# Differential attention in the even mixer: units 3 to 5 steps apart, and the second map scaled on ScalarE

## The reference

```python
def diff_attention_group(q, k, v, pos, layer, lambdas, subln):
    ...                                   # rope on q and k, 8 heads, two maps each of 64 dimensions
    lam = exp(sum(lf[0] * lf[1])) - exp(sum(lf[2] * lf[3])) + lam_init
    def block(start, q1b, q2b):           # 128 queries at a time
        mask = chunk_causal_mask(start, s)
        p1 = masked_softmax(einsum('bqhd,bkhd->bhqk', q1b, k1) * scale, mask)
        p2 = masked_softmax(einsum('bqhd,bkhd->bhqk', q2b, k2) * scale, mask)
        return einsum('bhqk,bkhe->bqhe', p1 - lam * p2, vf)
    o = sweep_query_blocks(block, q1, q2)
    return rms_norm(o, subln) * (1.0 - lam_init)
```

## Time and profile before

| | us |
|---|---|
| median of 3 runs | 2914.96 (2914.41 to 2916.4) |
| profiled execution, span | 2910.3 |
| around the span (median less span) | 4.7 |
| PE busy | 2814.2 |
| DVE busy | 1394.9 |
| ACT busy | 846.7 |
| POOL busy | 1355.7 |

### The profile page before, as it was taken

One profiled execution on the slowest core, in us unless ns is written; L12 is line 12 of the kernel. 1 busy time (PEld: TensorE's weight loads), 2 busy tenths in 40 slices (PEclk: granted clock), 3 DMA queues, 4 the chain that ended last, 5 costly groups with the idle time before them and its releaser, 6 DMA issues.

```text
span 2910.3 us, 36762 instructions
## 1 busy us (share of the span) xinstructions
PE 2814.2 (97%) x14588; PEld 2179.5 (75%) x14588; DVE 1394.9 (48%) x2266; ACT 846.7 (29%) x1575; POOL 1355.7 (47%) x1106
## 2 busy tenths in 40 slices
PE   7999999999989999999999999999999988999997
PEld 5888777777878877677886666788787755788886
DVE  3321656766563122435846777523725956511113
ACT  3011432331131143322336233232233225222222
POOL 3344323324534643558766543844545412744443
PEclk9999999999999999999999999999999989999999
DMA  7112222222321221233221112232323320332322
GB/s 269 44 44 66 66 66 94 69 78 94 122 76 59 68 77 58 73 101 119 87 73 57 57 47 73 76 101 83 105 81 100 126 59 16 118 99 86 103 85 74
DMA packets 244821, 243.81 MB, mean 84 GB/s; under 512 B 5376, under 2 KB 234624, under 8 KB 244032
## 3 DMA queue, kind: packets, MB, share of 16 engines
q1 hardware_dynamic: 243360, 237.96, 25.2%
q0 software_dynamic: 1312, 3.80, 0.5%
HBM read 233.22 MB, written 7.34 MB: 83 GB/s over the span
## 4 chain that ended last, share of the span: by engine, by line
PE 82%; DVE 11%; issue 2%; ACT 2%; POOL 1%; SPq 1%; DMA 1%; DVEq 0%; ACTq 0%; POOLq 0%
PE psum L933 22%; PE psum L935 21%; PE psum L934 21%; PE psum L1203 4%; PE psum L1182 1%; PE psum L1138 1%; DVE columns L2640 1%; PE psum L1158 1%; PE psum L1320 1%; PE psum L1137 1%; POOL columns L3352 1%; PE psum L1207 1%; DVE columns L2913 1%; PE psum L1471 1%; SPq L774 1%
## 5 line engine op out<-in xcount | busy, mean ns | idle before, releaser
L933 PE MATMUL psum<-columns,columns 128*128 128x512 f32 (+1 forms) x3464 | 1347.6, 389 | 12.6 <-POOL columns L3352 5.0
L935 PE MATMUL psum<-columns,columns 128*128 128x512 f32 (+1 forms) x3464 | 1263.2, 365 | 0.0
L934 PE MATMUL psum<-columns,columns 128*128 128x512 f32 (+1 forms) x3464 | 1261.7, 364 | 0.0
L3352 POOL TENSOR_TENSOR columns<-columns,columns 128x512 fp32r<-128x512 f32 (+1 forms) x676 | 912.3, 1379 | 436.6 <-ACT columns L1867 403.3
L3348 POOL TENSOR_TENSOR columns<-columns,columns 128x512 fp32r<-128x512 f32 x392 | 419.1, 1100 | 1011.0 <-PE psum L935 805.9
L933 PEld LDWEIGHTS psum<-columns,columns 128*128 128x128 f32 x3464 | 654.9, 189 | 196.1 <-issue 77.3
L934 PEld LDWEIGHTS psum<-columns,columns 128*128 128x128 f32 x3464 | 655.6, 189 | 124.3 <-issue 28.3
L935 PEld LDWEIGHTS psum<-columns,columns 128*128 128x128 f32 x3464 | 653.9, 189 | 111.5
L1867 ACT ACTIVATE columns<-columns 128x1024 fp32r<-128x1024 f32 (+2 forms) x154 | 136.7, 935 | 172.3 <-PE psum L935 165.8
L2640 DVE SCALAR_TENSOR_TENSOR columns<-columns,columns,columns 128x256 f32<-128x256 f32 x224 | 154.7, 745 | 0.0
L2622 DVE SCALAR_TENSOR_TENSOR columns<-columns,psum 128x512 f32<-128x512 f32 x80 | 54.7, 684 | 184.4 <-PE psum L1203 181.9
(11 more groups left out here) (414 smaller groups left out, 2754.8 us busy)
## 6 DMA issues: line engine op xcount, KB each, us to landing
columns<-in_w_merge SPq DMA_DIRECT2D x32, 1024.0 KB, 6.5
columns<-in_w_ada SPq DMA_DIRECT2D x24, 1024.0 KB, 5.7
columns<-in_w_in SPq DMA_DIRECT2D x22, 1024.0 KB, 5.1
columns<-in_ev_w_in SPq DMA_DIRECT2D x22, 1024.0 KB, 5.0
columns<-in_ffn_gate SPq DMA_DIRECT2D x22, 1024.0 KB, 5.2
columns<-in_ffn_up SPq DMA_DIRECT2D x22, 1024.0 KB, 5.2
columns<-in_ffn_down SPq DMA_DIRECT2D x16, 768.0 KB, 4.6
columns<-in_ffn_down SPq DMA_DIRECT2D x16, 640.0 KB, 4.1
```

What stands on the lines that cost most here:

```text
L933: mm(dst, weights(0, k), moving(0, k), start=start and k == 0, stop=False)
L934: mm(dst, weights(0, k), moving(1, k), start=False, stop=False)
L935: last = mm(dst, weights(1, k), moving(0, k), start=False, stop=stop and k == k_tiles - 1)
L3352: last = g.tensor_tensor(low[:, c], raw[:, c], high[:, c].bitcast(F32), ALU.subtract)
```

## The change

The fixed distance of 4 steps goes. The units start at 36 + 16h + (0, 3, 7, 11): three steps after unit 0 of a head, four after units 1 and 2, five from unit 3 to the next head. `turn` stays 8 steps and `mix` 11 steps behind. The exps are issued two steps after the scores. `swap` and `rope` of every second tile (n odd) stand at k = 1 in place of 2. The copy of a head's output, its square, its sum and what follows stand some steps further from `mix`, and since the units begin sooner and the last one starts at step 159 in place of 164, they are at about the same places as before or some steps earlier.

The scaling of the second map leaves DVE. `inverses(u)` on DVE inverts both sums and multiplies the second one's inverse by the factor; `scale(u)` on ACT multiplies the second map with it; `weights(u)` on DVE waits for that and adds. DVE's list at the start of unit u is now inverses(u - 1), maxima(u), weights(u - 1).

```diff
-UNIT_AT, UNIT_STEPS, TURN, MIX = 40, 4, 8, 11
+UNIT_STARTS = [36 + 16 * h + (0, 3, 7, 11)[i] for h, i in UNITS2]
+EXPS, TURN, MIX, LAST_WEIGHTS = 2, 8, 11, UNIT_STARTS[-1] + 5
...
-    return head_mixed_at(3) + 7 + 3 * h if h < 4 else head_mixed_at(7) + 7 + 2 * (h - 4)
+    return head_mixed_at(3) + 9 + 3 * h if h < 4 else head_mixed_at(7) + 9 + 2 * (h - 4)
...
-                    if k == 2 and 1 <= n <= 16:
+                    if k == 2 - n % 2 and 1 <= n <= 16:
                         swap(n - 1)
                     for h in range(8):
-                        if step == head_mixed_at(h) + 3:
+                        if step == head_mixed_at(h) + 5:
                             sub_sum(h)
...
+                def scale(u):
+                    n = (UNITS2[u][1] + 1) * P
+                    p = pr_diff[0][:, u % 2, 1, 0:n]
+                    act.wait_ge(total_inverted, UNITS0[2] + u + 1)
+                    f(p, p, ACT.Identity, scale=cols[:, 5 + 2 * (u % 2):6 + 2 * (u % 2)]).then_inc(prob_weighed, 1)
...
+                    u = unit2_at(step, 0)
+                    if u:
+                        scale(u - 1)
+                    if step == LAST_WEIGHTS:
+                        scale(len(UNITS2) - 1)
...
-                    u = unit2_at(step, 0)
+                    u = unit2_at(step, EXPS)
                     if u is not None:
                         exps(u)
                     for h in range(8):
-                        if step == head_mixed_at(h):
+                        if step == head_mixed_at(h) + 3:
                             act.wait_ge(o2_used, h + 1)
...
-                        if h % 4 == 3 and step == head_mixed_at(h) + 4:
+                        if h % 4 == 3 and step == head_mixed_at(h) + 6:
                             sub_root(h // 4)
...
-                def weights(u):
-
-                    n = (UNITS2[u][1] + 1) * P
+                def inverses(u):
                     c = cols[:, 4 + 2 * (u % 2):6 + 2 * (u % 2)]
                     dve.wait_ge(p2_ready, u + 1)
                     order(v.reciprocal(c, c))
+                    v.tensor_scalar(c[:, 1:2], c[:, 1:2], lamw[:, 5:6], None, ALU.mult).then_inc(total_inverted, 1)
+
+                def weights(u):
+
+                    n = (UNITS2[u][1] + 1) * P
+                    c = cols[:, 4 + 2 * (u % 2):6 + 2 * (u % 2)]
                     p = pr_diff[0][:, u % 2, :, 0:n]
-                    order(v.tensor_scalar(p[:, 1], p[:, 1], c[:, 1:2], lamw[:, 5:6], ALU.mult, ALU.mult))
+                    dve.wait_ge(prob_weighed, UNITS0[2] + u + 1)
...
                     u = unit2_at(step, 0)
                     if u is not None:
+                        if u:
+                            inverses(u - 1)
                         maxes(u)
                         if u:
                             weights(u - 1)
...
-                        if step == head_mixed_at(h):
+                        if step == head_mixed_at(h) + 2:
                             dve.wait_ge(mixed2, 4 * h + 4)
```

More of the change, by code:

```diff
@@ L308, in unit2_at @@
 def unit2_at(step, phase):
-    u = step - UNIT_AT - phase
-    return u // UNIT_STEPS if u >= 0 and u % UNIT_STEPS == 0 and u // UNIT_STEPS < len(UNITS2) else None
+    return UNIT_STARTS.index(step - phase) if step - phase in UNIT_STARTS else None
 def head_mixed_at(h):
-    return UNIT_AT + UNIT_STEPS * (4 * h + 3) + MIX
+    return UNIT_STARTS[4 * h + 3] + MIX
 def spread_at(h):
-    return head_mixed_at(3) + 7 + 3 * h if h < 4 else head_mixed_at(7) + 7 + 2 * (h - 4)
+    return head_mixed_at(3) + 9 + 3 * h if h < 4 else head_mixed_at(7) + 9 + 2 * (h - 4)
 OD_TILES = (4, 5, 6, 7, 8, 9, 0, 1, 2, 3)
@@ L2914, in maxes @@
                     v.tensor_scalar(c, c, -0.125, None, ALU.mult).then_inc(maxed2, 1)
+                def inverses(u):
+                    c = cols[:, 4 + 2 * (u % 2):6 + 2 * (u % 2)]
+                    dve.wait_ge(p2_ready, u + 1)
+                    order(v.reciprocal(c, c))
+                    v.tensor_scalar(c[:, 1:2], c[:, 1:2], lamw[:, 5:6], None, ALU.mult).then_inc(total_inverted, 1)
                 def weights(u):
@@ L2962, in ev_qk_out @@
                             weights(u - 1)
-                    if step == UNIT_AT + UNIT_STEPS * len(UNITS2):
+                    if step == LAST_WEIGHTS:
+                        inverses(len(UNITS2) - 1)
                         weights(len(UNITS2) - 1)
                     for h in range(8):
-                        if step == head_mixed_at(h):
+                        if step == head_mixed_at(h) + 2:
                             dve.wait_ge(mixed2, 4 * h + 4)
                             v.tensor_copy(qk2[:, h, :], psum[:, 7 * BANK:8 * BANK]).then_inc(o2_used, 1)
-                        if h % 4 == 3 and step == head_mixed_at(h) + 4:
+                        if h % 4 == 3 and step == head_mixed_at(h) + 6:
                             dve.wait_ge(sub_summed, h + 1)
```

2 lines of the change are left out of this document (removed).

## The result

The changed kernel takes 2923.8 us (median of 11 runs, 2920.7 to 2926.9), the kernel before 2916.0 on the same chip (11 runs, 2914.0 to 2918.7): ratio 1.0024, 95% interval 1.0016 to 1.0032. It is slower by 7.8 us. The prediction said 2923.0.

A forecast was written before the change was run, and what follows sets the result against it. TensorE, busy 97%, was taken as the bound, with 23.5 us at most to gain. Pauses of 26.5 us instead of 20.2 (6.3 more) plus 1.7 for the clock gave 8.0: 2914.96 + 8.0 = 2923.0 us, range 2910 to 2932.

The forecast's parts named there:

- (5): Start, first unit at step 36: TensorE waits 5.9 us behind VectorE's gate-norm multiply and first maxima, 4.5 us more.
- (3): GpSimd's windows, steps 48 to 96: one wait of 2.4 us each before unit 3's transposes, instead of 2.1 in two.
- (4): Odd tiles' ropes one step earlier: swap waits 0.15 us for ScalarE's copy, eight times, 1.2 us; lower end 0.
- (6): Later windows: 3.2 us lost at step 112, 4.6 at 128, 2.0 at 144, none at 160.
- (1): Second map's scaling on ScalarE: at most 0.72 us per unit, costing nothing as long as VectorE's maxima last longer.
- (2): One-column multiply added on VectorE per unit: 0.2 us and no wait for GpSimd; bounds 0.15 and 0.98.
- One fall more than before: Clock falls behind the start, step 112 and step 128, three instead of two: 1.7 us more.
- are nearer to 1.99 than to 2.90: Window waits of 2.4 us (shown as 2.3) bring no clock fall; a 1.99 pause kept full speed, 2.90 did not.
- The fall behind step 112: One of three expected clock falls, behind the waits at step 112 that add up to about 3.2 us.
- the rival of the clock in each window: Five more clock falls, behind four waits of 2.3 us and one of 2.0: 8.5 us, 2931 us; chance 15%.
- The faster rival: Unit 3's chain leaves GpSimd's window, saving 1.8 us in each of six windows: 2910.7 us; chance 20%.
- The start rival: First maxima come 4 us sooner, so the start costs nothing: 2916.8 us, no measurable change; chance 15%.

The follow-up runs named there:

- the run with the gate multiplies spread: Changed kernel with gate-norm multiplies 4 to 7 moved from steps 30 to 36 to steps 58, 74, 90 and 106; 2917.8 us.
- the run with short pieces: Changed kernel with GpSimd's splits of this stage in pieces of 256 instead of 512 elements; 2907.4 us (the same on the kernel before: 2907.5 us).
- the kernel with the scaling alone: Kernel before with only the second map's scaling moved to ScalarE, units still four steps apart from step 40; 2912.8 us.
- the kernel with both ropes behind the window in the new table: Changed kernel with both ropes of a head at steps 9 and 13, unit 3's weights before the next maxima, four gate-norm multiplies later; 2905.4 us.
- the even rope at step 5: Changed kernel with swap and rope of the even tiles at step 5 of the tile instead of 2; 2919.4 us.

## Why the prediction was right, and where it was not

The direction was right, and so were the places and causes of nearly all pauses. That the time came out to 0.8 us (2923.0 against 2923.8) is luck: the idle time was put too high by 4.8 us, the clock too low by 2 to 3, and 2.4 us of the measured difference lie outside the stage that the sum was made for.

*Idle time.* The prediction gave 6.3 us more lost in pauses. The trace gives 1.5: 20.1 us shown instead of 17.5 outside the wait of L1454, less 0.16 for each of seven pauses fewer (9 instead of 16). Term by term:

- (5), the start: 5.9 expected, 5.39 shown and 0.16, so 5.55. Right, and shown by the run with the gate multiplies spread.
- (3), the windows: 2.4 each expected, in one piece before the transposes of unit 3. They are there and in one piece, but lose 1.86 to 1.95 and 0.16, about 2.07, no more than two pauses lost before (2.0 to 2.1 by the prediction's count, 2.6 in the first window). The terms of that chain add up to 12.11, where 12.15 is written. The rope in the chain took 3.0 us (1694.03 to 1697.03) instead of the 3.45 of the earlier trace rows. Mis-sized by 0.3 each.
- (4), the odd ropes: 1.2 expected, nothing found. PE shows no pause in front of L1460, and undoing the move changes nothing. The lower end, 0, was the right one.
- (6), the later windows: steps 112, 128 and 144 were put at 3.2, 4.6 and 2.0; shown are 1.35 + 1.03, 3.85 and 0.89, with 0.16 for each about 2.7, 4.0 and 1.05. Order and causes were right, all three were too large, step 144 by half.
- (1) and (2), scaling and one-column multiply: ACT's scaling of 512 columns takes 0.72, the nearest form's time, and 0.21 is what the multiply costs, in POOL's window too (all 32 of them, a mean of 214 ns). In the whole stage DVE waits 0.9 us for ACT's scalings. Both as predicted.

That the multiply has no wait also answers the place in the Trainium skill ("VectorE: DVE Perf Modes", "What auto-detection actually checks") which, read strictly, would have made it wait: this trace disagrees with that reading, 0.21 at 1697.23 while POOL works. On the other place ("SBUF — State Buffer", "SBUF: two separate sides"), that one whole instruction holds the shared port, the run with short pieces agrees: POOL's instructions with half the columns take 0.73 to 0.82 us in that window instead of 1.20 to 1.44, and the wait in the multiply-add, over the 0.75 that it takes with POOL idle, goes from 1.08 to 0.44.

*The clock.* One fall more than before, 1.7 us, was the forecast. The stage has 20.4 us at the lower level instead of 6.8. Priced by the heads, 1.3 to 1.6 us for 3.4 of work, and leaving out the 2.8 and 1.2 us of the first and the last stretch in which PE had nothing to do anyway, that is 6.3 to 7.7 us instead of 2.6 to 3.2: an estimate of 3.7 to 4.5 more. The step that failed is the sentence that 2.3 us "are nearer to 1.99 than to 2.90": behind pauses of only 1.86 and 1.95 the clock fell twice out of four times in after, and four times out of four with the gate multiplies spread. The row of 1.99 could not decide it either. The same pause stands before L1454 in the kernel with the scaling alone, 1.98 long, and there the clock fell behind it, as it did in the kernel with both ropes behind the window in the new table; in the seven others that have it, it did not. The windows view of the stretch that begins 1.3 us behind L1454's resumption, in the first kernel and in after:

```profile
1594.10:1597.50 3.40, 3.40 (x9) 2.14 (x7) 0.00 (x0) 0.51 (x1) 3.40 (x3) 0.50 0.00 0
1592.20:1595.60 3.40, 3.40 (x15) 2.44 (x14) 0.00 (x0) 1.10 (x2) 3.40 (x3) 1.00 0.00 0
```

What decides it stays open. The fall behind step 112 that was expected did not come. So the rival of the clock in each window, at 15%, is half of what happened, at a smaller price per fall than the 1.7 that it was given.

1.5 + 3.7 = 5.2, with the upper price 6.0, and the stage is longer by 5.4, where the prediction had 8.0. The 4.7 us between span and median are no fixed cost either: in the timed runs the difference of time and span is 1.9, so the profiled execution of before was simply a quick one. The forecast does not hang on it, as it adds to the median. In the profile of after the odd mixer has one more stretch at the lower level. The windows view of it:

```profile
2470.30:2477.10 6.80, 5.96 (x37) 4.21 (x36) 3.20 (x11) 2.92 (x8) 3.80 (x4) 0.50 0.01 2
```

Other kernels (the even rope at step 5, the short pieces on after) have it too, others not, and nothing in the change reaches there. What brings it about stays open.

*The faster rival.* It needed POOL to be done before the multiply-add of unit 3. POOL ended at 1702.28, one microsecond after it. It was refuted for this kernel, yet its mechanism is the one that paid: shortening POOL's instructions gains 16 us, and moving the ropes out of their reach 18, some 6 of which the gate multiplies bring, which that kernel spreads too. *The start rival* was refuted by the 5.39.

## What to carry to other kernels

Before moving units so that more steps lie between them, mark the stretch in which the neighbour engine on the shared port works, and count what each table puts into it; here the two scalings in that stretch made 21.9 of the 27.3 us that the table costs without the move to ACT, while no gain by the spacing itself was measured. Where an engine waits for one whole instruction of another, shorten the other's instructions before moving anything: halving them gained 8 us in one table and 16 in the other, though they make the other engine slower. A wait that is put into an in-order queue (ACT's for the inverses) costs what stands behind it, here a copy that had nothing to do with it. And look at where a gain arises, not only at its size: the move of the even ropes gained 4.4 us, but none in the heads whose pauses it was to shorten.

## What the runs showed of the hardware

Three things that I had not expected:

- A POOL split of 512 elements is cheaper per element than of 256 (10.6 against 12.4 us for a panel), and dearer for the kernel.
- A stretch of 3.4 us at 1.2 GHz costs 1.3 to 1.6 us of a head, not 1.7.
- In after the clock fell behind one pause of 1.86 us (1725.08) and one of 1.95 (1701.21) and not behind others of the same lengths (1678.51, 1655.90); with the gate multiplies spread it fell behind all four. I had taken it as decided by the length of the pause.
